# A streaming retention encoder layer on eight cores: rotated keys of heads two to four transposed by DMA instead of by TensorE

## The reference, cut to what matters

```python
q = rotary(q.reshape(B, L, H_RET, DK_HEAD).astype(jnp.float32), pos)
k = rotary(k.reshape(B, L, H_RET, DK_HEAD).astype(jnp.float32), pos) * (DK_HEAD ** -0.5)
...
def step(S, qkv):
    qc, kc, vc = qkv
    s = jnp.einsum('bihd,bjhd->bhij', qc, kc) * intra_dec[None]
    o = jnp.einsum('bhij,bjhe->bihe', s, vc)
    o = o + jnp.einsum('bihd,bhde->bihe', qc, S) * inter_dec[None, :, :, None]
    S = S * carry_dec[None, :, None, None] + jnp.einsum(
        'bjhd,bjhe->bhde', kc * upd_dec[None, :, :, None], vc)
    return S, o
```

## Time and profile before

| | us |
|---|---|
| median of 3 runs | 1610.19 (1608.97 to 1610.97) |
| the profiled execution, its own time | 1609.0 |
| its span on the slowest core (core 6) | 1608.0 |
| spans of the eight cores | 1604.7 to 1608.0 |
| TensorE busy | 1570.3 |
| VectorE busy | 804.2 |
| ScalarE busy | 468.2 |
| GpSimd busy | 258.0 |

### The profile page before, as it was taken

One profiled execution on the slowest core, in us unless ns is written; L12 is line 12 of the kernel. 1 busy time (PEld: TensorE's weight loads), 2 busy tenths in 40 slices (PEclk: granted clock), 3 DMA queues, 4 the chain that ended last, 5 costly groups with the idle time before them and its releaser, 6 DMA issues.

```text
span 1608.0 us, 27355 instructions; the slowest of 8 cores (1604.7 to 1608.0 us)
## 1 busy us (share of the span) xinstructions
PE 1570.3 (98%) x9222; PEld 876.1 (54%) x9310; DVE 804.2 (50%) x1510; ACT 468.2 (29%) x923; POOL 258.0 (16%) x468
## 2 busy tenths in 40 slices
PE   5999999999999999999999999999999999999997
PEld 2555566655664455556665566445555566556653
DVE  3566673256222856668424622276666852472226
ACT  1555521113110055552111311005555211131100
POOL 2122211012110322221101210022222110021102
PEclk9999999999999999999999999999999999999999
DMA  9945865569863698587565986369955877578521
GB/s 186 154 79 92 170 111 86 85 119 190 148 100 54 125 192 185 103 200 113 86 98 105 185 144 105 53 131 177 204 119 110 154 138 114 87 137 144 101 45 79
DMA packets 61671, 201.17 MB, mean 125 GB/s; under 512 B 6880, under 2 KB 8544, under 8 KB 61536
## 3 DMA queue, kind: packets, MB, share of 16 engines
q0 software_dynamic: 40752, 149.70, 58.5%
q1 hardware_dynamic: 20208, 48.66, 9.2%
q10 hardware_dynamic: 576, 1.05, 0.3%
HBM read 329.11 MB, written 19.96 MB: 217 GB/s over the span
## 4 chain that ended last, share of the span: by engine, by line
PE 89%; DVE 6%; issue 3%; DMA 1%; POOL 1%; ACT 0%; DVEq 0%; ACTq 0%; POOLq 0%
PE P L934 19%; PE P L552 14%; PE P L818 12%; PE P L739 11%; PE P L991 9%; PE P L840 8%; PE P L517 7%; PE P L692 2%; PE P L640 2%; PE P L897 2%; DVE sb_stat L866 1%; PE P L670 1%; DMA sb_xT<-xT 1%; DVE sb_RA L900 1%; POOL sb_stat L876 1%
## 5 line engine op out<-in xcount | busy, mean ns | idle before, releaser
L934 PE MATMUL P<-sb_R,sb_W 128*128 128x384 bf16 x2112 | 345.2, 326 | 0.0
L934 PEld LDWEIGHTS P<-sb_R,sb_W 128*128 128x128 bf16 x2112 | 206.3, 98 | 135.7
L188 POOL DMA_DIRECT2D sb_W<-wb x278 | 152.4, 552 | 759.4 <-PE P L934 281.5
L552 PE MATMUL P<-sb_W,sb_xT 128*128 128x512 bf16 x1072 | 251.1, 379 | 2.0 <-issue 0.4
L739 PE MATMUL P<-sb_xT,sb_W 128*128 128x384 bf16 x1152 | 196.0, 326 | 0.0
L552 PEld LDWEIGHTS P<-sb_W,sb_xT 128*128 128x128 bf16 x1104 | 106.0, 98 | 121.0 <-issue 2.8
L517 PE MATMUL P<-sb_xT,sb_W 128*128 128x384 bf16 x768 | 143.7, 333 | 18.3 <-ACT sb_xT L1031 10.6
L739 PEld LDWEIGHTS P<-sb_xT,sb_W 128*128 128x128 bf16 x1152 | 110.9, 98 | 72.1 <-issue 1.2
L833 DVE TENSOR_TENSOR sb_scr<-P,sb_scr 128x384 f32<-128x384 f32 x96 | 53.2, 556 | 192.6 <-PE P L840 160.9
L939 ACT ACTIVATE sb_scr<-P 128x384 f32<-128x384 f32 x132 | 64.4, 490 | 242.8 <-PE P L934 242.8
L818 PE MATMUL P<-sb_xT,sb_W 128*128 128x384 bf16 x768 | 133.1, 326 | 0.0
(11 more groups left out here) (96 smaller groups left out, 1696.0 us busy)
## 6 DMA issues: line engine op xcount, KB each, us to landing
sb_W<-wb POOLq DMA_DIRECT2D x278, 512.0 KB, 9.9
sb_xres<-xp SPq DMA_DIRECT2D x16, 512.0 KB, 12.2
sb_xres<-sret SPq DMA_DIRECT2D x16, 512.0 KB, 15.3
ss_o<-sb_xres SPq DMA_DIRECT2D x16, 512.0 KB, 8.9
yp<-sb_RA SPq DMA_DIRECT2D x15, 512.0 KB, 3.1
sb_lnp<-lnp SPq DMA_DIRECT2D x12, 512.0 KB, 10.1
sb_xT<-xT POOLq DMA_DIRECT2D x5, 768.0 KB, 15.9
sb_cst<-cs SPq DMA_DIRECT2D x6, 384.0 KB, 8.5
```

The costliest lines, as they stand in the source:

```text
L188: self.E[q].dma_start(out=o, in_=i).then_inc(self.dsem[key], 16)
L552: S.pe([(lambda kc=kc: nc.tensor.matmul(P[b][:, :], xtile(s, kc, t), ws[kc // 4][:, kc % 4, :], start=(kc == 0), stop=(kc == 7)), [wc_(s, ...
L934: S.pe([(lambda kc=kc: nc.tensor.matmul(P[b][:, 0:n], w[:, kc, ji * 128:ji * 128 + 128], hT(kc, c0, c0 + n), start=(kc == 0), stop=(kc == 7)),
```

## The change

The keys of heads two to four (`h` = 1, 2, 3) are no longer transposed by TensorE. When `rope` has written a half block of rotated keys, SyncE issues one transposing DMA from `kT` to a new buffer `kraw`, 128 partitions by 768 elements of bf16. `kraw` has one half for each parity of the head, and it shares its memory with `lnp`, the parameters of LayerNorm, which are loaded after the four heads. `k_tr` of these heads is the ScalarE instruction alone, now from `kraw` instead of PSUM. `kT` is laid out tile by tile, so that a half block is one stretch. Head one (`h` = 0) keeps the transposes on TensorE.

```diff
--- before.py
+++ after.py
@@ -177,7 +177,7 @@
         self._record(tok, set(allr), writes)
         return tok
 
-    def dma(self, q, key, pairs, reads=(), writes=()):
+    def dma(self, q, key, pairs, reads=(), writes=(), turn=False):
         if key not in self.dsem:
             self.dsem[key] = self.es.enter_context(self.nc.semaphore("dsem_" + key))
             self.dcnt[key] = 0
@@ -185,7 +185,7 @@
             self._wait(q, ("d_" + key, self.dsem[key], self.dcnt[key]))
         self._sync(q, reads, writes)
         for (o, i) in pairs:
-            self.E[q].dma_start(out=o, in_=i).then_inc(self.dsem[key], 16)
+            (self.E[q].dma_start_transpose if turn else self.E[q].dma_start)(out=o, in_=i).then_inc(self.dsem[key], 16)
             self.dcnt[key] += 16
         tok = ("d_" + key, self.dsem[key], self.dcnt[key])
         self._record(tok, reads, writes)
@@ -342,7 +342,8 @@
         goTc = [[V3(RA, 32 * c0, 16, n, BF16) for (c0, n) in CHUNKS[s]] for s in range(NST)]
         hh = V3(RA, 0, NT, 1024, F32)
         qT = [V3(SET[i], 0, 2, TS, BF16) for i in range(2)]
-        kT = [V3(SET[i], 3072, 2, TS, BF16) for i in range(2)]
+        kT = [V3(SET[i], 3072, NT, 256, BF16) for i in range(2)]
+        kraw = [V3(LNP, 3072 * i, NT, 256, BF16) for i in range(2)]
         vv = [V3(SET[i], 6144, NT, 512, BF16) for i in range(2)]
         gg = V3(GG, 0, 3, 512, BF16)
         kp = V3(KP, 0, 2, 256, BF16)
@@ -530,7 +531,14 @@
             r = [scr(i, 0, n) for i in sl]
             rc = [scr.c(i) for i in sl]
             t1, t2 = P[b1][:, 0:n], P[b2][:, 0:n]
-            dst = (kT if which == "K" else qT)[h % 2]
+            m = n // 128
+            t0 = c0 // 128
+
+            def dst(hf):
+                if which == "Q":
+                    return qT[h % 2](hf, c0, c0 + n), lambda a: a, qT[h % 2].c(hf, c0, c0 + n)
+                o = hf * 128
+                return (kT[h % 2]((t0, t0 + m), o, o + 128), lambda a: a.rearrange("p (a b) -> p a b", a=m), kT[h % 2].c((t0, t0 + m), o, o + 128))
 
             def tt(o, a, b, op, rd, wr):
                 S.op("dve", lambda: nc.vector.tensor_tensor(out=o, in0=a, in1=b, op=op), reads=rd, writes=wr)
@@ -540,8 +548,13 @@
             tt(r[1], t2, sin, ALU.mult, [f"P{b2}", cn], [rc[1]])
             tt(r[3], t2, cos, ALU.mult, [f"P{b2}", cc], [rc[3]])
             rel(b2)
-            tt(dst(0, c0, c0 + n), r[0], r[1], ALU.subtract, [rc[0], rc[1]], [dst.c(0, c0, c0 + n)])
-            tt(dst(1, c0, c0 + n), r[2], r[3], ALU.add, [rc[2], rc[3]], [dst.c(1, c0, c0 + n)])
+            for hf, (x, y, op) in enumerate(((0, 1, ALU.subtract), (2, 3, ALU.add))):
+                d, view, dc = dst(hf)
+                tt(d, view(r[x]), view(r[y]), op, [rc[x], rc[y]], [dc])
+            if which == "K" and h > 0:
+                ks, kd = kT[h % 2], kraw[h % 2]
+                S.dma("sp", f"kt{h % 2}{t0}", [(kd.full[:, t0:t0 + m, :].rearrange("p a (u b) -> p (a u) b", u=2), ks.full[:, t0:t0 + m, :].rearrange("p a b -> p (a b)"))],
+                      reads=[ks.c((t0, t0 + m))], writes=[kd.c((t0, t0 + m))], turn=True)
 
         def mm_tok(s, t, name, h):
             b = bank()
@@ -593,13 +606,16 @@
 
 
         def k_tr(s, h, t):
+            hs = h % 2
+            kind = tiles[s][t]["kind"]
+            if h > 0:
+                S.op("act", lambda: nc.scalar.activation(out=kp(t % 2), in_=kraw[hs](t), func=AF.Identity, scale=vec(kind, h, h + 1)),
+                     reads=[kraw[hs].c(t), vec.c()], writes=[kp.c(t % 2)])
+                return
             b = bank()
-            hs = h % 2
             pb = P[b][:].bitcast(BF16)
-            tt = (t * 128, t * 128 + 128)
-            S.pe([(lambda hf=hf: nc.tensor.transpose(pb[:, hf * 128:(hf + 1) * 128], kT[hs](hf, *tt), idb(0)),
-                   [kT[hs].c(hf, *tt), idb.c()]) for hf in range(2)], [f"P{b}"])
-            kind = tiles[s][t]["kind"]
+            S.pe([(lambda hf=hf: nc.tensor.transpose(pb[:, hf * 128:(hf + 1) * 128], kT[hs](t, hf * 128, hf * 128 + 128), idb(0)),
+                   [kT[hs].c(t, hf * 128, hf * 128 + 128), idb.c()]) for hf in range(2)], [f"P{b}"])
             S.op("act", lambda: nc.scalar.activation(out=kp(t % 2), in_=pb[:, 0:256], func=AF.Identity, scale=vec(kind, h, h + 1)),
                  reads=[f"P{b}", vec.c()], writes=[kp.c(t % 2)])
             rel(b)
@@ -608,8 +624,8 @@
             b = bank()
             hs = h % 2
             tt = (t * 128, t * 128 + 128)
-            S.pe([(lambda hf=hf: nc.tensor.matmul(P[b][:, 0:128], kT[hs](hf, *tt), qT[hs](hf, *tt), start=(hf == 0), stop=(hf == 1)),
-                   [kT[hs].c(hf, *tt), qT[hs].c(hf, *tt)]) for hf in range(2)], [f"P{b}"])
+            S.pe([(lambda hf=hf: nc.tensor.matmul(P[b][:, 0:128], kT[hs](t, hf * 128, hf * 128 + 128), qT[hs](hf, *tt), start=(hf == 0), stop=(hf == 1)),
+                   [kT[hs].c(t, hf * 128, hf * 128 + 128), qT[hs].c(hf, *tt)]) for hf in range(2)], [f"P{b}"])
             kind = tiles[s][t]["kind"]
             S.op("dve", lambda: nc.vector.tensor_tensor(out=sTm(t % 2), in0=P[b][:, 0:128], in1=maskt(kind * 4 + h), op=ALU.mult),
                  reads=[f"P{b}", maskt.c(kind * 4 + h)], writes=[sTm.c(t % 2)])
```

## The result

The changed kernel takes 1631.57 us (median of 4 runs, 1629.23 to 1634.18) against 1609.58: ratio 1.0137, 95% interval 1.0119 to 1.0154. It is 22 us slower; 41 were forecast. The profiled execution took 1634.2 us, with spans of 1624.2 to 1633.1 us on the eight cores.

What follows compares the result with a forecast made beforehand. TensorE, busy 98% of the span, was taken as the bound. 1609.0 - 5.8 (removed transposes) + 43.5 (two stalls) + 3.0 (clock) = 1649.7, or 1651 as the median, standing 1.2 us higher; range 1615 to 1680 us.

Steps and rivals of the forecast that it cites:

- R + 4.3: Stages 1 and 2: L646 on TensorE starts 4.3 us of ScalarE work after `kp` is released; delay 21.7 and 21.8 us.
- the projections up to 611.5: Stage 1: TensorE's remaining work ahead of L646, taken as already contained in L646's earlier start at 611.8.
- R: Release of `kp` of tile 0 on ScalarE: 629.2 in stage 1 instead of 604.12, and 1156.1 in stage 2.
- So I let the transfer begin to move at 624.2: Stage 1, hardware queue: served in order, so the keys' transfer starts when the second load of states lands, at 624.2.
- I take 5 us: Transfer time of a half block of keys once it moves, assuming no weights are asked for while TensorE stands.
- The transfer's own time: Half block of keys: lower bound 2.1 us (256 KB store, quiet queue), upper bound 23 us (768 packets), taken as 5.
- 15 us and more to land in stage 0: Stated sign: if the transposes take this long to land in stage 0, the prediction is wrong in its size.
- The clock: TensorE's granted clock is lower after each of two stalls: 1.5 us lost per stall, 3 us in all.
- both stalls between 12 and 32 us: 1632 to 1670: The main forecast for the stalls in stages 1 and 2; chance 0.68.
- the second rival: Transposes overtake the loads or share the engines: R = 611.1, 3.6 us per stall, 1613; in between up to 1628; chance 0.12.
- A faster kernel: Third rival: `kp` comes before TensorE runs out of work, no stall, 1604.4 us; break-even at R = 610.4; chance 0.05.
- The transfer is slow in itself: First rival: transfer takes 23 us instead of 5, delay of 40 us per stage, 1711 us; chance 0.15, from 1670 on.

Runs made afterwards that it cites:

- second experiment: The changed kernel, but head two keeps its transposes on TensorE and only heads three and four go by DMA: 1607.44 us, ratio 0.9969 to the kernel before.
- first experiment: The changed kernel, but the load of states for head h+2 is issued at the end of the step, behind the keys' transposing DMA: 1625.31 us, ratio 1.0091.
- sixth experiment: The changed kernel, but states are stored and loaded at the end of step 2, behind both transposing DMAs of the head: 1609.27 us, ratio 0.9995.
- third experiment: The changed kernel, with a plain copy of the same bytes in place of each transposing DMA: 1628.68 us, ratio 1.0111.

## Why the prediction was right, and where it missed

**Direction, place and mechanism held.** The removed pairs were priced at 5.8 us; without any transfer the kernel gains 6.9 (5.0 to 8.9). The transposing DMA of head two stood behind the loads, which waited for the stores, as the earlier trace rows said; issue at 607.8 was forecast at about 609 less 2. `kp` was the instruction that waited, once in stage 1 and once in stage 2 and nowhere else.

**The step from release to L646 agrees by luck.** "R + 4.3" gives 618.3 + 4.3 = 622.6, and L662 started at 622.62. But the 4.3 us were ScalarE's way to the casts, and these ended at 622.25; L662 waited for nothing. What came last was TensorE's own projection, which I had as already done ("the projections up to 611.5"). It had not run, for want of the PSUM bank that the value copy frees, started at 619.54, and took 2.72 us at the lower clock instead of 1.46.

**The step that was mis-sized is R.** R, the release of `kp`, was put together from "So I let the transfer begin to move at 624.2", where the second load should land, and "I take 5 us". It was 618.3 instead of 627 (629.2 less the 2 us of stage 0). The load landed at 617.4 and the transfer 0.8 us behind it. The first term was read from a trace in which nobody stood; in the second I had the missing weights in view and still took 5 us, where the trace has 0.8. What ends the weights' traffic is not that TensorE stands, as the forecast had it, but that `kp` holds ScalarE, and ScalarE holds GpSimd, which issues the weights: 19.2 us without an issue, from before TensorE stood. So the weights' queue ran dry at 616, and then the hardware queue moved alone. With no stall the same load took 14.4 to 16.9 us (second experiment, eight cores), with it 8.6 to 10.7. In the changed kernel the keys land some 2 us after that point, and in the first experiment at 616.4, where the weights' queue had moved its last packets by 616. I read from this that the end of the stall is where the weights' queue runs dry, and that the changed kernel (ScalarE waits 14.1 us) and the order in which SyncE was not held by the loads (11.8 us) differ little for that reason; no run that lets GpSimd issue the weights during the stall was made to test it.

**The transfer's own time** was put between 2.1 and 23 us. Both ends exist: 2.7 us from issue to landing at quiet places, 16 us and more beside the weights (sixth experiment). Behind the load, on a queue without weights, it landed after 0.8 us more, which is below my lower bound. The upper bound, 768 packets of 256 bytes one for one with the weights', was the right picture; I used it for a rival only, and took a middle. My own sign for a wrong size, "15 us and more to land in stage 0", came true: 20.0 us, and up to 30.1 in the sixth experiment, beyond my upper bound. It cost nothing in the changed kernel, as stage 0 has some 25 us to spare. The order of the queue was right too. The Trainium skill (VectorE: DVE Perf Modes, The three transpose paths) gives 1309 ns for one block by DMA, an estimated 7.9 us for six. Here the same six blocks took from 2.7 to 20.0 us to land in one kernel: the traffic beside them decides.

**The clock** was put at 1.5 us for a stall. On core 4 of the kernel before, L646 of the two stages:

```profile
608.91 0.63 PE L646 MATMUL P<-sb_Sbf,sb_hset 128*64 128x512 bf16 x4
...
1135.68 0.63 PE L646 MATMUL P<-sb_Sbf,sb_hset 128*64 128x512 bf16 x4
```

From one to the other it takes 526.8 us; in the changed kernel, on the same core, from 622.62 to 1161.71, 539.1. The 12.3 us more are the second stall's 9.8, less 18 pairs (1.9), plus what the first stall's clock cost: 4.4 us. The rows show a first part at 0.50 and a second at 0.81. I had read the loss from a gap of 4 us. Worked out in the same way, the other cores give 2.6 to 4.7 us.

**The sum** with the measured terms: -5.8 + 9.5 + 9.8 (stalls) + 2 x 4.4 (clock) = +22.3, against +22.0 of the medians. Forecast were -5.8 + 43.5 + 3.0. That it meets to 0.3 us is luck: the two stalls come to between 15.1 and 19.6 us by core, and core 4 of the profiled execution also began 4.8 us later than in the profile before (first key transposes at 47.69 us against 42.85), before the first transposing DMA; why is not shown.

**The rivals.** The measured time lies within the stated range, but beside the scenario to which I gave 0.68 ("both stalls between 12 and 32 us: 1632 to 1670"): the stalls were 9.5 and 9.8 us, and 1631.6 falls between it and the upper end of the second rival (1628). "The transposes overtake the loads" did not happen; the loads themselves came sooner. A faster kernel needed R under 610.4. "The transfer is slow in itself" is half true: in the first experiment it makes 7 of the 11.8 us of the wait, and in the sixth its 16 us and more make the keys late together with the loads ahead of it. In the changed kernel as it stands the place alone suffices (third experiment). So there are two causes. The place behind the states' stores and loads is enough by itself. The 768 small packets beside the weights can be late by themselves too, but by little: in stage 0 of the sixth experiment `kp` waited up to 4.7 us and TensorE up to 0.8, and in stage 0 of the changed kernel nobody waited. Keeping head two on TensorE where states are swapped avoids both.

What stays open: whether a lighter weight burst at the start of a stage would let head two's keys come in time, and whether the stall would grow if GpSimd's weight loads did not stand behind ScalarE's square sum. Neither was tried.

## What to carry to other kernels

A DMA that takes over work from a busy engine has a due time: before it is put in, look up what waits ahead of it on its issuing engine, then what is ahead of it in the hardware queue, then how many packets it has and how many each of them must share with. Bytes are a bad measure for a transposing DMA beside a stream of big packets; count packets. And when a stall is priced from a trace without it, follow the wait to the engines that issue the other traffic: if they are held too, that traffic stops, and the stall ends sooner than the rows without it say. The clock after the stall can cost more than a shorter gap suggests: here about 4 us for each stall of 9.5 us.

## What the runs showed of the hardware that was not expected

- A transposing DMA of 128 x 768 bf16 moves as 768 packets of 256 bytes, and 32 more. Beside the weights' packets, 3.6 KB each on average (2.82 MB in 773), it goes one for one, 44 to 48 a us: 197 KB in 16 us and more. With the weights' queue at 60 packets in 2 us, it moved 588; with none there, the hardware queue moved 1408 (0.53 MB, a load's tail among them) from 616 to 618 us in the changed kernel. At quiet places the whole took 2.7 us from issue to landing.
- Issuing it holds SyncE for 1.2 us in most cases and once for 4.9 us; a plain one, such as the loads of `lnp` elsewhere, for some 0.4. Minimum, median and maximum in ns, changed kernel:

```profile
L188 SPq DMA_TRANSPOSE sb_lnp<-sb_hset x18: 1211/1248/4907, 58.0 to 1224.6; - x18
L188 SPq DMA_DIRECT2D sb_lnp<-lnp x12: 328/433/1053, 196.7 to 1463.3; - x12
```

- After a stall of 9.5 us TensorE worked at the lower clock level for some 4 us, was granted 0.98 and 1.00 for 8, and then 0.81 for 12 us while busy throughout.
- ScalarE's instruction of 256 columns took 500 ns from SBUF and 468 ns from PSUM.
